# A mixer with three gate pairs ahead of its inner gates, and GpSimd's work in pieces of 256 columns

## The reference, cut to what matters

```python
def rg_lru(xs, wa, ba, wx, bx, lam):
    r = sigmoid(einsum('bsnd,nde->bsne', xb, wa) + ba)
    i = sigmoid(einsum('bsnd,nde->bsne', xb, wx) + bx)
    log_a = 8.0 * r * log_sigmoid(lam)
    a = exp(log_a)
    mult = sqrt(-expm1(2.0 * log_a))
    b = mult * (i * xs)
    h = linear_scan(a, b)            # h[t] = a[t] * h[t-1] + b[t]
    return h

def recurrent_mixer(xn, w_in, conv_w, conv_b, ...):
    gate_branch, rec_branch = split(xn @ w_in, 2)
    gate = gelu(gate_branch, approximate=True)
    rec = causal_depthwise_conv(rec_branch, conv_w) + conv_b      # 4 taps
    return (gate * rg_lru(rec, ...)) @ w_out
```

## Time and profile before

| | us |
|---|---|
| median of 3 runs | 2378.35 |
| lowest, highest | 2376.0, 2382.14 |
| the profiled execution | 2381.23 |
| its span | 2379.4 |
| PE busy in it | 2197.1 (92%) |
| DVE busy | 1550.9 (65%) |
| ACT busy | 1201.6 (50%) |
| POOL busy | 39.2 (2%) |

### The profile page before, as it was taken

The page is one execution under the profiler, slowest core; times in us unless marked ns, Lnnn a source line. Parts: engine busy times, 40 slices in busy tenths (PEclk is TensorE's granted clock), DMA queues, the critical chain, the costliest instruction groups (busy, mean ns, idle before and its releaser), DMA issues.

```text
span 2379.4 us, 29321 instructions
## 1 busy us (share of the span) xinstructions
PE 2197.1 (92%) x11070; PEld 1847.0 (78%) x11070; DVE 1550.9 (65%) x2056; ACT 1201.6 (50%) x1588; POOL 39.2 (2%) x35
## 2 busy tenths in 40 slices
PE   5589999997999999999799998499997899999999
PEld 4368888786877888778798888488875688898887
DVE  8986558887537656888765557855555555466554
ACT  3134457775453545777435444654445454445443
POOL 4100000000000000000000000000000000000000
PEclk9789999998999999999899999799998999999999
DMA  5134668996503457999455554345541255545652
GB/s 217 36 115 159 204 222 318 351 346 238 188 9 142 160 187 242 354 347 348 167 190 181 179 194 132 116 163 190 186 159 62 106 189 186 192 158 171 194 194 98
DMA packets 123004, 451.52 MB, mean 190 GB/s; under 512 B 13808, under 2 KB 13808, under 8 KB 121968
## 3 DMA queue, kind: packets, MB, share of 16 engines
q1 hardware_dynamic: 121536, 442.03, 53.9%
q0 software_dynamic: 1040, 6.82, 0.8%
q10 hardware_dynamic: 288, 0.81, 0.1%
HBM read 448.55 MB, written 1.05 MB: 189 GB/s over the span
## 4 chain that ended last, share of the span: by engine, by line
PE 77%; DVE 13%; ACT 4%; DMA 3%; issue 3%; SPq 0%; ACTq 0%; DVEq 0%
PE bank L302 20%; PE bank L304 20%; PE bank L303 20%; DVE w_lo L278 4%; DMA raw<-in_stream 3%; PE bank L295 3%; PE bank L296 3%; PE bank L297 3%; ACT w_hi L271 1%; DVE scr L2398 1%; DVE scr L2413 1%; PE bank L615 1%; DVE scr L1656 1%; PE bank L1048 1%; DVE scr L2405 1%
## 5 line engine op out<-in xcount | busy, mean ns | idle before, releaser
L278 DVE TENSOR_TENSOR w_lo<-raw,w_hi 128x1024 fp32r<-128x1024 f32 x829 | 989.8, 1222 | 534.6 <-ACT w_hi L271 529.1
L271 ACT ACTIVATE w_hi<-raw 128x1024 fp32r<-128x1024 f32 x839 | 876.1, 1059 | 711.9 <-PE bank L304 544.6
L302 PE MATMUL bank<-w_hi,x_hi 128*128 128x512 f32 (+1 forms) x1056 | 414.4, 392 | 8.6 <-DVE x_lo L515 8.6
L303 PE MATMUL bank<-w_lo,x_hi 128*128 128x512 f32 (+1 forms) x1056 | 411.0, 389 | 0.0
L304 PE MATMUL bank<-w_hi,x_lo 128*128 128x512 f32 (+1 forms) x1056 | 411.0, 389 | 0.0
L302 PE MATMUL bank<-w_hi,c_hi 128*128 128x512 f32 x906 | 359.4, 397 | 52.2 <-issue 23.1
L304 PE MATMUL bank<-w_hi,c_lo 128*128 128x512 f32 x906 | 356.6, 394 | 0.0
L303 PE MATMUL bank<-w_lo,c_hi 128*128 128x512 f32 x906 | 356.3, 393 | 0.0
L302 PEld LDWEIGHTS bank<-w_hi,c_hi 128*128 128x128 f32 x906 | 172.6, 191 | 93.8 <-issue 48.4
L302 PEld LDWEIGHTS bank<-w_hi,x_hi 128*128 128x128 f32 x1056 | 199.6, 189 | 49.4 <-issue 5.6
L295 PE MATMUL bank<-x_hi,w_hi 128*128 128x256 f32 x736 | 213.0, 289 | 20.7 <-DVE w_lo L278 16.9
(11 more groups left out here) (400 smaller groups left out, 2088.4 us busy)
## 6 DMA issues: line engine op xcount, KB each, us to landing
raw<-in_stream SPq DMA_DIRECT2D x839, 512.0 KB, 4.3
ln_rows<-in_ln POOLq DMA_DIRECT2D x4, 1024.0 KB, 4.9
scr<-in_xt SPq DMA_DIRECT2D x1, 1024.0 KB, 5.1
scr<-in_s POOLq DMA_DIRECT2D x1, 1024.0 KB, 10.6
x<-in_x POOLq DMA_DIRECT2D x1, 1024.0 KB, 5.2
out_x<-x SPq DMA_DIRECT2D x4, 256.0 KB, 2.7
par<-in_par ACTq DMA_DIRECT2D x1, 765.5 KB, 10.4
ln_rows<-in_ple POOLq DMA_DIRECT2D x1, 512.0 KB, 12.3
```

The costliest lines, as they stand in the source:

```text
L271: nc.scalar.activation(w_hi[:, n % RING, :], raw[:, n % RING, :], ACT.Copy).then_inc(hi_done, 1)
L278: nc.vector.tensor_tensor(w_lo[:, n % RING, :], raw[:, n % RING, :], w_hi[:, n % RING, :].bitcast(F32), ALU.subtract).then_inc(lo_done, 1)
L302: nc.tensor.matmul(out, xh, hi, start=start, stop=False)
L303: nc.tensor.matmul(out, xh, lo, start=False, stop=False)
```

## The change

In the mixer:

- PE's fills: five rec, **three** gates (into banks 5, 6, 7), the inner gates (banks (2g + j) % 8), two gates (banks 2, 3). The order of the weights in the stream changes with it.
- The first tap of the convolution (multiply and add the bias) moves from DVE to ACT.
- DVE takes `c_lo` of group g - 1 of the inner gates in group g, behind its two splits.
- a squared is a second Exp on ACT, with scale 2, in place of a product on DVE.
- Gelu of gates 0 to 2 stands ahead of the tanhs, that of 3 and 4 behind the roots.
- `rest_of_c` of the output stands one group behind the gating, no longer behind all of them.
- The constants of the decay and the half bias are computed in the ffn stage ahead of the mixer (`lru_setup_act`, `lru_setup_dve`); `decay` moves to another buffer for it.
- The places of the splits are spread anew.

In S5:

- GpSimd splits a tile in four operations of 256 columns, and computes each level's sum group by group (255 columns and fewer).
- `yg_lo(0, 2)` moves from ahead of the second scan to behind the issue of its second step.
- `add_skip(3, 1)`, a split and `yg_lo(3, 1)` stand ahead of the lo part of the embedding's input (`p_lo`, L2505), no longer behind it.

The diff, cut to its core:

```diff
@@ ffn_act, ffn_dve
             rms_act(act, st)
+            if st + 1 < len(stages) and stages[st + 1][0] == "lru":
+                lru_setup_act(act, st + 1)
...
+                    if u == 1 and st + 1 < len(stages) and stages[st + 1][0] == "lru":
+                        lru_setup_dve(dve, st + 1)
@@ lru_pe
-            fill("gate", 0, 5)
+            for g in range(3):
+                fill("gate", g, lru_gate_bank(g))
...
-                    b = psum[(6 + 2 * g + j) % 8]
+                    b = lru_inner_bank(g, j)
...
-            for g in range(1, LG):
-                fill("gate", g, lru_gate_fill(g))
+            for g in range(3, LG):
+                fill("gate", g, lru_gate_bank(g))
@@ lru_act
             for g in range(LG):
+                act.wait_ge(dve_did["rec"], dve_did.at("rec", st, g))
+                for c in (2 * g, 2 * g + 1):
+                    last = nc.scalar.activation(lru_x[:, c, :], lru_in[:, c, 0:T], ACT.Identity,
+                                                bias=column("lru_conv_b", c), scale=column("lru_conv_w", c))
+                last.then_inc(act_did["inner hi"], act_did.next("inner hi", st, "first tap", g))
                 split_hi(act)
...
-            split_hi(act)
-            split_hi(act)
+            for g in range(3):
+                split_hi(act)
+                gelu(g)
             act.wait_ge(dve_did["half bias"], dve_did.at("half bias", st))
...
-                if g in (1, 4):
-                    split_hi(act)
+                if g in (1, 3):
+                    split_hi(act, 1)
             for g in range(LG):
                 act.wait_ge(dve_did["log a"], dve_did.at("log a", st, g))
-                link(act, "act", nc.scalar.activation(pair(lru_a, g), pair(lru_r, g), ACT.Exp))
+                nc.scalar.activation(pair(lru_a, g), pair(lru_r, g), ACT.Exp)
+                link(act, "act", nc.scalar.activation(pair(lru_x, g), pair(lru_r, g), ACT.Exp, scale=2.0))
...
-                if g < 2:
-                    split_hi(act)
+                if g in (0, 2):
+                    split_hi(act, 1)
...
-            for g in range(LG):
-                act.wait_ge(dve_did["gate"], dve_did.at("gate", st, g))
...
+            split_hi(act)
+            for g in range(3, LG):
+                gelu(g)
             for g in range(LG):
                 round_c(act, st, g, pair(lru_x, g), "dve", ("gated", st, g))
+                if g in (1, 2, 3):
+                    split_hi(act, 1)
@@ lru_dve
             for g in range(LG):
...
+                if g:
+                    split_lo(dve)
+                    inner_lo(g - 1)
+                dve.wait_ge(act_did["inner hi"], act_did.at("inner hi", st, "first tap", g))
+                for tap in range(1, 4):
...
+            split_lo(dve)
+            inner_lo(LG - 1)
+            for g in range(3):
+                gate(g)
+                split_lo(dve)
...
+                if g in (1, 3):
+                    split_lo(dve, 1)
 
             for g in range(LG):
                 dve.wait_ge(act_did["a"], act_did.at("a", st, g))
-                v(nc.vector.tensor_tensor(pair(lru_x, g), pair(lru_a, g), pair(lru_a, g), ALU.mult))
                 nc.vector.scalar_tensor_tensor(pair(lru_x, g), pair(lru_x, g), 1.0, pair(lru_r, g), ALU.add, ALU.mult).then_inc(
                     dve_did["minus b2"], dve_did.next("minus b2", st, g))
-                if g < 3:
-                    gate(g + 1)
-                if g < 2:
-                    split_lo(dve)
-            gate(4)
+                if g in (0, 2):
+                    split_lo(dve, 1)
+                if g in (2, 4):
+                    gate(3 if g == 2 else 4)
+            split_lo(dve)
             v(nc.vector.memset(lru_a[:, :, 0:1], 0.0))
...
-            for g in range(LG):
-                rest_of_c(dve, st, g, pair(lru_x, g))
+                if g:
+                    rest_of_c(dve, st, g - 1, pair(lru_x, g - 1))
+                if g > 1:
+                    split_lo(dve, 1)
+            rest_of_c(dve, st, LG - 1, pair(lru_x, LG - 1))
             split_lo(dve, lead_of(st + 1) - dve_at.tile)
@@ s5_dve, scan
                     else:
+                        if half == 1 and c == 1:
+                            yg_lo(0, 2)
                         v(ins)
...
-            yg_lo(0, 2)
             scan(1)
...
             yg_lo(2, 1)
+            add_skip(3, 1)
+            split_lo(dve, 1)
+            yg_lo(3, 1)
             dve.wait_ge(act_did["start hi"], act_did.at("start hi", "p"))
             nc.vector.scalar_tensor_tensor(p_lo[:, :, :], ple_raw, 0.5, p_hi[:, :, :].bitcast(F32), ALU.mult, ALU.subtract).then_inc(
                 dve_did["start lo"], dve_did.next("start lo", "p"))
-            add_skip(3, 1)
-            yg_lo(3, 1)
-            split_lo(dve, 1)
@@ s5_pool
-                    nc.gpsimd.tensor_tensor(w_lo[:, n % RING, :], raw[:, n % RING, :], w_hi[:, n % RING, :].bitcast(F32),
-                                            ALU.subtract).then_inc(lo_done, 1)
+                    for quarter in range(4):
+                        at = slice(quarter * T, quarter * T + T)
+                        last = nc.gpsimd.tensor_tensor(w_lo[:, n % RING, at], raw[:, n % RING, at], w_hi[:, n % RING, at].bitcast(F32),
+                                                       ALU.subtract)
+                    last.then_inc(lo_done, 1)
...
-                v(nc.gpsimd.tensor_tensor(dst[:, g, w:], src[:, g, w:], src[:, g, 0:T - w], ALU.add))
+                for g in range(level, 4):
+                    last = nc.gpsimd.tensor_tensor(dst[:, g, w:], src[:, g, w:], src[:, g, 0:T - w], ALU.add)
+                v(last)
```

More of the change, by code:

```diff
@@ L1604, in lru_act, with gelu @@
                     act_did["inner hi"], act_did.next("inner hi", st, g))
-            split_hi(act)
-            split_hi(act)
+            def gelu(g):
+                act.wait_ge(dve_did["gate"], dve_did.at("gate", st, g))
+                nc.scalar.activation(pair(lru_gate, g), pair(lru_gate, g), ACT.Gelu_apprx_tanh).then_inc(
+                    act_did["gelu"], act_did.next("gelu", st, g))
+            for g in range(3):
+                split_hi(act)
+                gelu(g)
             act.wait_ge(dve_did["half bias"], dve_did.at("half bias", st))
@@ L1634, in lru_act, with lru_setup_dve @@
             split_hi(act, lead_of(st + 1) - act_at.tile)
[L1636 removed]
+        def lru_setup_dve(dve, st):
             def v(ins):
                 link(dve, "dve", ins)
[L1640 to L1674 removed]
@@ L1688, in lru_dve, with v, inner_lo, gate @@
             v(nc.vector.scalar_tensor_tensor(decay, acc, -8.0, e, ALU.mult, ALU.add))
-            for g in range(LG):
+            v(nc.vector.tensor_scalar(half_bias[:, 0:LC], column("lru_ba", 0, LC), 0.5, None, ALU.mult))
+            nc.vector.tensor_scalar(half_bias[:, LC:2 * LC], column("lru_bx", 0, LC), 0.5, None, ALU.mult).then_inc(
+                dve_did["half bias"], dve_did.next("half bias", st))
+        def lru_dve(dve, st):
+            def v(ins):
+                link(dve, "dve", ins)
+            split_lo(dve)
+            v(nc.vector.memset(lru_in[:, :, 0:3], 0.0))
+            rms_dve(dve, st)
+            spread_dve(dve, st, psum[7])
+            def inner_lo(g):
+                dve.wait_ge(act_did["inner hi"], act_did.at("inner hi", st, g))
+                nc.vector.tensor_tensor(pair(c_lo, g), pair(lru_x, g), pair(c_hi, g).bitcast(F32), ALU.subtract).then_inc(
+                    dve_did["inner lo"], dve_did.next("inner lo", st, g))
+            for g in range(LG):
+                dve.wait_ge(pe_did["rec"], pe_did.at("rec", st, g))
+                nc.vector.tensor_tensor(lru_in[:, 2 * g:2 * g + 2, 3:], bank(psum[g]), over_pair(rstd[:, :]), ALU.mult).then_inc(
+                    dve_did["rec"], dve_did.next("rec", st, g))
+                dve.wait_ge(dve_did["rec"], dve_did.at("rec", st, g))
+                if g:
[3 more added lines that the diff above has]
+                for tap in range(1, 4):
+                    for c in (2 * g, 2 * g + 1):
+                        src, dst, w = lru_in[:, c, tap:tap + T], lru_x[:, c, :], column("lru_conv_w", tap * LC + c)
+                        last = nc.vector.scalar_tensor_tensor(dst, src, w, dst, ALU.mult, ALU.add)
+                    if tap < 3:
+                        v(last)
+                last.then_inc(dve_did["convolved"], dve_did.next("convolved", st, g))
+                dve.wait_ge(dve_did["convolved"], dve_did.at("convolved", st, g))
+            def gate(g):
+                dve.wait_ge(pe_did["gate"], pe_did.at("gate", st, g))
+                nc.vector.tensor_tensor(pair(lru_gate, g), bank(lru_gate_bank(g)), over_pair(rstd[:, :]), ALU.mult).then_inc(
+                    dve_did["gate"], dve_did.next("gate", st, g))
+            split_lo(dve)
[3 more added lines that the diff above has]
+                split_lo(dve)
+            for g in range(LG):
```

(2 more changed lines are left out.)

71 lines of the change are left out of this document (17 added, 54 removed).

## The result

The changed kernel took **2358.8 us** (median of 4; 2355.1 to 2359.1) against 2378.5 for the kernel before in the same set of runs: ratio 0.9908, 95% interval 0.9895 to 0.9921. A second set gave 2356.4 against 2379.0, ratio 0.9909 (0.9892 to 0.9925). The profiled execution has a span of 2357.2 against 2379.4, 22.2 less.

A forecast was written before the change was run, and what follows sets the result against it. TensorE has 77% of the chain, so gains come only where it stands still; VectorE sets the time there. Mixer 19.2 plus S5 5.6 give 24.8 us: 2381.2 to 2356.4, median 2353.5, range 2348 to 2361.

The forecast's parts named there:

- ScalarE's two taps: Mixer, conv loop: group 0 waits for ScalarE's multiply and bias add, put at 0.7 to 1.1 us, taken as 0.9.
- the setup's 3.4 us: Mixer: decay setup (3.1 us) and half bias (0.3) leave the path, costing nothing in the ffn stage before.
- part two: S5, four GpSimd tiles beside rotations 4 to 7: quarters cut waits of 5.1 us, gain 3.0 (2.3 to 3.7).
- yg_lo: S5: moving yg_lo(0, 2) behind scan 1's second step removes VectorE's 1.32 wait for ScalarE, gain 1.3 us.
- the rival, 0 without cover: S5: yg_lo's move gains 0 if the cover, TensorE's 2.75 us idle before the next read-outs, fails; no chance given.
- add_skip: S5: putting add_skip(3) ahead of p_lo gains nothing, bounds -0.2 and 0.5 us.
- part one: S5, rotations 0 to 3: quarters gain 4.5 us, small operations give some back; net 0.6 to 3.5, taken as 1.3.
- GpSimd's quarter: S5: a quarter of a split tile on GpSimd takes 0.71 us, a tile 2.83, 0.5 more than whole.
- Rival 1: S5: quarters gain nothing, small operations pay what rotations save; 2358.5 us, chance 0.14.
- Rivals 2 and 3: Mixer: 2, ten table loads for one in the exponentials, 2365, chance 0.04; 3, TensorE starves in fills, 2403.2, chance 0.03.
- Rival 4: Mixer: output product waits for a bank or tile, not c_lo 0; only S5's 5.6 us come, 2372.8, chance 0.02.
- the 9.3 and the 3.4: Mixer: TensorE's idle us before the inner gates of groups 3 and 4, forecast to vanish along with the low clock.

The follow-up runs named there:

- experiment 5: Changed kernel with the decay's setup and the half bias back in the mixer; 2354.8 us in one run, first rec drain to output product 75.85 us against 75.84.
- experiment 6: Kernel before with GpSimd's quarter splits alone: 2379.1 us, S5 107.05; and with S5's change except yg_lo's move: 2371.8, S5 106.68 (before 110.41, S5's part 105.11).
- experiment 7: Kernel before with S5's whole change, GpSimd's splits in eighths instead of quarters; 2377.6 us in one run, S5 104.28 us against 105.11.
- experiment 4: Changed kernel with one gate pair ahead of the inner gates: 2361.4 us, mixer 80.80; separately, with the old conv loop: 2362.5, mixer 81.61 (changed kernel 75.84).
- experiment 2: Changed kernel with the two splits behind the roots put later, behind group 0's rounding and c_lo 0; 2348.2 us, ratio 0.9872, mixer 70.46.

## Why the prediction was right

**The mixer: right, term by term.** 19.2 forecast, 19.18 on the trace. All of S5's and the experts' gain lies ahead of the mixer, so the prediction's times are to be read 4.98 us earlier:

| step | forecast, less 4.98 | measured |
|---|---|---|
| conv group | 6.34 | 6.35 |
| last c_lo of the conv loop done | 1479.7 | 1479.9 |
| first tanh | 1487.5 | 1487.62 |
| tanhs end | 1496.8 | 1496.90 |
| exponentials end | 1508.6 | 1508.7 |
| VectorE's idle before the splits | 3.7 | 3.67 |
| first root product | 1516.0 | 1516.17 |
| output product | 1522.1 | 1522.13 |

One table load more, as said (four from 1479 to 1515, three before), and a single pause of 17.4, not 17.6. A small term was off: ScalarE's two taps take 1.09 together (0.55 each), the upper bound and not the 0.9 taken; two splits of VectorE cover that in all groups but the first. The mechanism held; that the sum hits to 0.02 is luck, since the steps are off by 0.1 to 0.2 each, and the 95.02 itself is one execution (94.89 to 96.04 in four others with the old mixer). One reading was wrong without any effect on the sum: the setup's 3.4 us were said to leave the path, and experiment 5 shows that in the new order they would not have been on it. The ffn stage did not notice the setup (from its first table load to the mixer's 189.56 before, 189.60 after).

**S5: 5.6 forecast, 5.2 measured.** The total is closer than its terms, which were off in both directions: part two 3.0, measured 3.3; yg_lo 1.3, measured 1.6 (the rival, 0 without cover, fell with experiment 6); add_skip 0, as forecast within 0.1; **part one 1.3, measured 0.5**. This is the term that was mis-sized. The rotations gained 5.4 (they end at 47.5 instead of 52.9), more than the 4.5 that I gave (L2404 and L2405 mean 0.77 and 1.22, where 0.9 to 1.1 stood for both); but the small operations and copies gave back 4.9 and not some 3: four copies that took 0.9 take 2.1, tensor_scalars of 0.29 take up to 0.69.

I had asked whether only operations with two SBUF tensors wait or copies too, and took 1.3 because no row showed a copy beside GpSimd. They wait too. The Trainium skill (GPSIMD Engine Reference, Key points) says that VectorE instructions in a 2-port perf mode contend with GpSimd as well as those with two SBUF inputs, and from copies and scans waiting I had worked out 0.6. The trace agrees that copies and tensor_scalars wait; that it gives 0.5, so near to 0.6, is luck, since gain and loss both came 0.9 larger than in that working. The scan steps, which have two SBUF inputs, take up to 1.55 beside GpSimd in experiment 7, against 1.22.

The other size that was off is GpSimd's quarter: 0.85 with its waits, not 0.71, because GpSimd also waits for VectorE, which the sum had only one way round. GpSimd's copy of eight columns shows it (timeline, changed kernel), first free, then beside VectorE's scan step of 57.14 to 58.44:

```profile
55.09 0.19 POOL L2575 COPY hidden_buf<-hidden_buf 128x8 f32<-128x8 f32 x1
57.42 1.00 POOL L2575 COPY hidden_buf<-hidden_buf 128x8 f32<-128x8 f32 x1
```

The row that the prediction read as VectorE alone (L2405 in 0.68) is a case of it: it was no gap of GpSimd, whose copy there took 0.67 and whose sum of 248 columns 1.15, against 0.19 and 0.70 in the changed kernel where nothing held them up. As the price of L2405 without a wait, 0.68 was right.

**The rivals.** Rival 1 (quarters gain nothing) is half true and told apart by experiment 6: nothing in the first part, 3.3 in the second. Rivals 2 and 3 did not show: one load ahead of the exponentials, and no pause between fills. Rival 4 did not either: c_lo 0 releases the product (7.8 us later when c_lo comes 7.8 later).

**The sum: 24.8 forecast, 24.4 on the trace (19.2 + 5.2), 19.8 and 22.6 by the medians.** The missing part lies in stages that nothing touched. The prediction had "a us or two of scatter" for it and put it on both sides of the range; against 134.2 before, eight of the other profiled executions had latent attention 1.3 to 3.5 us longer, with the old mixer and with the new. My reason for rival 3, that a pause is dear for the clock behind it, I had not applied to the value of the parts: the 9.3 and the 3.4 were counted as gone, with the right result, but experiment 4 shows that I could not have said what they were worth.

**What stays open**: how the 5.0 us of experiment 4 divide between the low clock and the order of the queues; what the second Exp is worth; and what decides in which executions latent attention meets the low clock.

## What to carry to other kernels

Where two engines in turn hold up a third, write their queues side by side with durations from the trace: a wait for a round trip then shows as a gap into which work of the next group fits, and the next thing that is late shows too (here it gave experiment 2, the best version). Price an idle matrix engine by the clock behind it and by whose queue holds the splits that wait for its tiles. Cutting a second engine's operations small helps where the first has few of the operations that contend, and moves the contention elsewhere where it has many: take the stretch behind it into the sum.

## What the runs showed that was not expected

The low clock at the head of a matmul burst behind a pause can last differently in two executions of the same program, and so does the same product. The first 5 us of the mixer's output product, in the changed kernel's two executions, both behind a pause of 17.38 us:

```profile
1522.13:1527.13 5.00, 5.00 (x15) 4.00 (x16) 3.93 (x5) 1.58 (x2) 0.00 (x0) 0.68 0.02 5
```

```profile
1519.07:1524.07 5.00, 5.00 (x12) 3.94 (x13) 3.93 (x5) 1.58 (x2) 0.00 (x0) 0.50 0.02 5
```

From its start to the next stage's L302 the product took 32.1 and 33.1 us. S5's output product, restarted at 134.4 to 134.9 in the kernels with S5's whole change, has its next table load at 144.7 in the changed kernel and at 142.6 with S5's part alone. Stretches from the changed kernel and from S5's part alone:

```profile
134.80:139.80 5.00, 4.95 (x15) 0.66 0.77 262
```

```profile
134.50:139.50 5.00, 5.00 (x23) 1.00 0.76 270
```

The work and the pause ahead (2.18 us in both) are the same; 15 and 23 matmuls in 5 us are not. From restart to load that is 9.8 and 8.3 us, 1.6 of scatter at one place. Several such places go with times of single executions that spread over 12 us (2374.9 to 2386.7 in 17 runs of the kernel before). Stretches of the trace with no such burst on their path agree within 0.1: the new mixer 75.81 to 75.85 in four executions, S5 with its whole change 105.1 to 105.2. The old mixer has a burst behind a pause inside it, and its stretch spreads over 1.1 us (94.89 to 96.04 in five).

A second GpSimd effect: its own operations lengthen beside VectorE. A quarter beside rotations 4 to 7 is 13.79 / 16 = 0.86 us, an eighth 16.87 / 32 = 0.53, so the fixed part of a piece is about 2 x 0.53 - 0.86 = 0.2 us there, waits included (an estimate), against 0.16 from the earlier trace rows, and a quarter is 0.15 longer than the 0.71 worked out from operations that stood alone.
